# Gate and up projections of the feed-forward in two halves of 256 tokens, each with its own loads of the stationary weights

## The reference

```
x = x + groups @ w_out
h2 = rms_norm(x, g_ffn)
return x + (silu(h2 @ w_gate) * (h2 @ w_up)) @ w_down        # first block
...
gu = h @ w_in                                                # layers 0 to 3
return (silu(gu[..., :2816]) * gu[..., 2816:]) @ w_out
```

## Time and profile before

| | |
|---|---|
| median of 2 runs | 3288.5 us (3285.84 to 3291.16) |
| profiled execution, first to last instruction | 3288.7 us |
| instructions | 42736 |
| TensorE matmuls | busy 3220.8 us (98%), 15181 |
| TensorE weight loads | busy 2619.6 us (80%), 15181 |
| VectorE, ScalarE, GpSimd | busy 47%, 37%, 45% |
| memory traffic | 114 GB/s over the span |

### The profile page before, as it was taken

One profiled execution on the slowest core, in us unless ns is written; L12 is line 12 of the kernel. 1 busy time (PEld: TensorE's weight loads), 2 busy tenths in 40 slices (PEclk: granted clock), 3 DMA queues, 4 the chain that ended last, 5 costly groups with the idle time before them and its releaser, 6 DMA issues.

```text
span 3288.7 us, 42736 instructions
## 1 busy us (share of the span) xinstructions
PE 3220.8 (98%) x15181; PEld 2619.6 (80%) x15181; DVE 1549.8 (47%) x2615; ACT 1202.1 (37%) x1875; POOL 1480.9 (45%) x724
## 2 busy tenths in 40 slices
PE   8999999999999999999999999999999999999998
PEld 6876788888778888887888878877888877788886
DVE  2453355501145555467555224656556354752223
ACT  3455333222335332455432243125332243553322
POOL 3540554454235445524544454446444453154442
PEclk9999999999999999999999999999999999999999
DMA  4400155532224554211556333113555322032331
GB/s 161 122 26 1 65 204 191 202 106 93 68 65 160 193 202 145 84 59 63 180 191 208 105 96 96 39 33 103 204 191 188 103 90 77 5 99 96 96 103 64
DMA packets 103107, 376.12 MB, mean 114 GB/s; under 512 B 11456, under 2 KB 11584, under 8 KB 102848
## 3 DMA queue, kind: packets, MB, share of 16 engines
q1 hardware_dynamic: 102816, 373.86, 34.1%
q0 software_dynamic: 160, 0.52, 0.1%
HBM read 372.24 MB, written 2.10 MB: 114 GB/s over the span
## 4 chain that ended last, share of the span: by engine, by line
PE 52%; DVE 2%; ACT 1%; issue 1%; POOL 0%; DVEq 0%; ACTq 0%
PE bank L758 13%; PE bank L757 13%; PE bank L756 13%; PE bank L1362 2%; PE bank L859 1%; PE bank L854 1%; PE bank L855 1%; PE bank L808 1%; PE bank L809 1%; PE bank L810 1%; PE bank L1072 1%; PE bank L1328 1%; PE bank L1089 0%; PE bank L974 0%; PE bank L1258 0%
## 5 line engine op out<-in xcount | busy, mean ns | idle before, releaser
L623 POOL TENSOR_TENSOR w_lo<-raw,w_hi 128x1024 fp32r<-128x1024 f32 x501 | 1227.3, 2455 | 1368.2 <-ACT w_hi L1440 1368.0
L1440 ACT ACTIVATE w_hi<-raw 128x1024 fp32r<-128x1024 f32 x501 | 526.8, 1057 | 1183.2 <-PE bank L758 1022.4
L756 PE MATMUL bank<-h_hi,w_hi 128*128 128x512 f32 x2280 | 889.3, 390 | 0.0
L758 PE MATMUL bank<-h_hi,w_lo 128*128 128x512 f32 x2280 | 887.1, 389 | 0.0
L757 PE MATMUL bank<-h_lo,w_hi 128*128 128x512 f32 x2280 | 887.0, 389 | 0.0
L756 PEld LDWEIGHTS bank<-h_hi,w_hi 128*128 128x128 f32 x2280 | 427.9, 188 | 90.6 <-issue 2.0
L757 PEld LDWEIGHTS bank<-h_lo,w_hi 128*128 128x128 f32 x2280 | 427.9, 188 | 89.7 <-issue 1.0
L758 PEld LDWEIGHTS bank<-h_hi,w_lo 128*128 128x128 f32 x2280 | 427.9, 188 | 89.2
L2608 DVE CUSTOM_DVE_ANT_0 ada_raw<-ada_raw,cond_row 128x1024 f32<-128x1024 f32 x192 | 304.2, 1587 | 280.5 <-DMA ada_raw<-ada 270.6
L756 PE MATMUL bank<-hid_hi,w_hi 128*128 128x512 f32 x880 | 344.0, 391 | 0.0
L758 PE MATMUL bank<-hid_hi,w_lo 128*128 128x512 f32 x880 | 342.4, 389 | 0.0
(11 more groups left out here) (411 smaller groups left out, 4016.5 us busy)
## 6 DMA issues: line engine op xcount, KB each, us to landing
raw<-weights SPq DMA_DIRECT2D x501, 512.0 KB, 3.5
ada_raw<-ada SPq DMA_DIRECT2D x192, 512.0 KB, 4.3
layer_const<-layer_const SPq DMA_DIRECT2D x5, 512.0 KB, 3.6
x<-x_t SPq DMA_DIRECT2D x1, 2048.0 KB, 7.5
cond_row<-cond SPq DMA_DIRECT2D x4, 512.0 KB, 4.2
y_t<-x SPq DMA_DIRECT2D x8, 256.0 KB, 2.0
tables<-big_const SPq DMA_DIRECT2D x1, 768.0 KB, 5.9
cols<-columns SPq DMA_DIRECT2D x1, 569.5 KB, 8.4
```

The lines of the kernel that those rows point to most:

```text
L623: nc.gpsimd.tensor_tensor(w_lo[k % RING][:, :, :], raw[k % RING][:, :, :], w_hi[k % RING][:, :, :].bitcast(F32), ALU.subtract).then_inc(sm ...
L756: mm(out, w_hi[r][:, at, :], hi, start=first and at == 0, stop=False)
L758: op = mm(out, w_lo[r][:, at, :], hi, start=False, stop=last and at == len(pairs) - 1)
L1440: fn(w_hi[t % RING][:, :, :], raw[t % RING][:, :, :], ACT.Copy).then_inc(sm.hi_done, 1)
```

## The change

`m_tile` gets a flag `halved`, and `linear` passes it on in its loop of four tiles. `ffn` sets it for the gate and up tiles. With it, an output tile is computed in two halves of 256 tokens: for the first half all 8 chunks with their three matmuls each, then the same for the second half, into the two halves of the same bank. A tile then has 48 matmuls of 256 columns, each with its own load of a 128 x 128 stationary piece, in place of 24 of 512 columns. The waits at the head of the tile and the increment on its last matmul stay. The early tiles, the tile after the loop and all other projections keep the form of before.

```diff
-            def m_tile(k, mt, i, step, mt_step, hi, lo, chunks, parts_from=None):
+            def m_tile(k, mt, i, step, mt_step, hi, lo, chunks, parts_from=None, halved=False):
                 if mt >= 4:
                     pe.wait_ge(sm.lin_free, mt - 3 + mt_step * i)
+                if halved:
+                    pe.wait_ge(sm.lo_done, k + 1 + step * i)
+                    r = k % RING
+                    for t in range(2):
+                        tok = slice(256 * t, 256 * t + 256)
+                        out = bank[mt % 4][:, tok]
+                        for c in range(DT):
+                            mm(out, w_hi[r][:, c, :], hi[:, c, tok], start=c == 0, stop=False)
+                            mm(out, w_hi[r][:, c, :], lo[:, c, tok], start=False, stop=False)
+                            op = mm(out, w_lo[r][:, c, :], hi[:, c, tok], start=False, stop=c == DT - 1)
+                    op.then_inc(sm.slot_used, 1)
+                    return
...
-            def linear(tiles, hi, lo, chunks, after_second=None):
+            def linear(tiles, hi, lo, chunks, after_second=None, halved=False):
...
-                            m_tile(k + (done + q) * per, mt + done + q, i, 4 * per, 4, hi, lo, chunks)
+                            m_tile(k + (done + q) * per, mt + done + q, i, 4 * per, 4, hi, lo, chunks,
+                                   halved=halved)
...
-                linear(2 * FT - EARLY, h_hi, h_lo, [8])
+                linear(2 * FT - EARLY, h_hi, h_lo, [8], halved=True)
```

## The result

The changed kernel takes 3353.1 us (median of two runs, 3352.90 and 3353.35) against 3288.5 us, a ratio of 1.0192 with a 95% interval of 1.0162 to 1.0222. A second comparison gave 3354.3 us (median of 4) against 3290.2 us (median of 7), 1.0190 (1.0173 to 1.0207). So the change makes the kernel 1.9% slower, 64 us; the forecast was 3298 us with a range to 3340 us.

The account below looks back on a forecast made before the run. TensorE, busy for 98% of the span, was taken as the bound: matmul count times pace. 4800 x 1.9 ns = +9.1 us on 3288.7 us, other terms nothing, gave 3298 us; range 3283 to 3340 us, held at 0.80.

Parts of the forecast that it names:

- Step (1): In the loop of `linear`, 4800 matmuls of 512 columns (1088 us) become 9600 of 256 with 9600 loads.
- Step (2): In the halved loops, a 256-column stream takes 114.3 ns, two 228.6 ns: +1.9 ns for each replaced matmul.
- Step (3): In the halved loops, load and stream overlap, the longer sets the pace: max(114.3, 111.7) = 114.3 ns a half.
- Its lower bound: For a half in the loops: 106.7 ns, with none of the 13.4 ns over 512 columns; -64 us.
- The first rival: In the halved loops, array hand-over adds 13.4 ns to the load: 125.1 ns a half, 3401 us; 3354 or more, chance 0.09.
- Steps (4) and (5): In the halved loops, issue, waits, other engines' work and TensorE's doubled weight reads cost nothing, hidden behind TensorE.
- The load that comes too late by a little: In the halved loops, 2.6 ns of room is too little for the load; +113 us, 3354 or more at chance 0.09.
- its small form: A smaller lateness of the load in the halved loops: 116 to 120 ns a half, 3313 to 3352 us, chance 0.09.
- Load and stream in turns: In the halved loops, load and stream partly or wholly alternate: 169 or 226 ns a half, 3826 or 4370 us; chance 0.03.
- Instructions fetched again: At 45 backward jumps, the body of 384 loads and matmuls waits 2.5 us for a block: +112 us, 3401 us; chance 0.03.
- A half is cheaper than half: In the halved loops, 106.7 ns a half gives 3225 us; below 3283 us chance 0.03, over 2% faster 0.01.

Follow-up runs that it names:

- the quarters: The changed kernel with each tile in four pieces of 128 columns instead of two of 256, loads still of 128 columns: 4349.7 us.
- The 320- and 384-column trains: Runs of 24 equal-length matmuls in the changed kernel, tiles cut into 320 and 192 or 384 and 128 columns instead of 256 and 256: 3445.9 and 3576.1 us.

## Why the prediction was wrong

- **Step (1)**, 9600 matmuls of 256 for 4800 of 512: right, 3200 on each of the three new lines.
- **Step (2)**, the stream of a half at 114.3 ns, +1.9 ns for each replaced matmul: this is the step that failed, by its size. It measured 120.0 ns, +13.3 ns, which is 63.8 us where the sum had 9.1. The step took the price from a row with loads of half the width, said so, and costed that difference at nothing; the run with 256 columns behind loads of 64 shows 113.3 ns in these very loops, and only the full width of the load, with the rows written that go with it, brings it to 120.0.
- **Step (3)**, the longer of stream and load: right for the load (111.7 ns, the quarters) and right in that loads are not paid in full. Its lower bound named the 13.4 ns over 512 columns and asked only what would happen if a half had none of them. The reading next to it, that a half has all of them, was not made: 106.7 + 13.4 = 120.1 ns, and the result to within 1 us. The first rival did use the 13.4 ns, but on top of the load (125.1 ns). The plain f32 row (215 ns for 256 columns, little over twice 106.7) could be read as a small price, and it is of another number type.
- **Steps (4) and (5)**, issue, waits and memory at nothing: right. TensorE has no idle time in the loops, and the other engines keep their room.
- **The load that comes too late by a little** came nearest in size: its small form reached to 3352 us. It held that handing over new weights takes time, which fits a fixed price, but it put that time behind the load, where a longer stream would cover it. The 320- and 384-column trains pay in full with 35 and 62 ns of room, and the 192-column steps of 111.8 ns leave no room for a hand-over behind the load. Its point of decision, 120.2 ns, happens to lie beside the 120.0 that another cause made.
- **Load and stream in turns** is refuted: 120.0 ns is far under 169. The Trainium skill (TensorE: Matmul & The Clock Gate, Part 3, "The mechanism"), by whose rule loads on the same row groups do not overlap a matmul, differs from this trace after as before. The same section also has a load pulled ahead that goes into the background weight buffer; whether these loads do, the trace does not say.
- **Instructions fetched again** is refuted: at most two blocks in a whole loop, and no longer step at a turn. The row it rested on, no block on q8 in the first loop, came from a stretch that ends before the loop does; over the whole loop (413.4 to 631.0 us) there is one, as in the second. The rule of the Trainium skill on jumps (Runtime: NRT & Kernel Launch, "Instruction fetch mechanics") differs from the trace: the quarters' body of 768 loads and matmuls is longer than two blocks of 256 however it lies, and no turn stalls. The same section's store of 2048 instructions is in keeping with that, though no run shows its size.
- **A half is cheaper than half** is refuted by the same 120.0 ns.
- **The range.** It ended at 3340 us within a case that reached to 3352; with 120.1 ns as one of the bounds of step (2) it would have held the time.

## What to carry to other kernels

Before a stream is cut into shorter ones, take the running step apart into columns at the granted clock and a rest, and cost the cut with the whole rest paid again for each piece as well as with none of it. A row that serves as a price must match in number type, stream length and load width; if one of them differs, that difference is a bound of the range and not nothing. An engine that is busy for 98% of the span turns every nanosecond of an inner step into time: here 13 ns, 4800 times.

## What the runs showed of the hardware

- In float32r with 128 x 128 loads at the 2.4 GHz level a step takes 120.0, 146.4, 173.0 and 226.7 ns for 256, 320, 384 and 512 columns, and 111 to 112 ns for 128 and 192 (without the first steps of uneven trains).
- At 256 columns the price of a step falls with the width of its load, 13.3, 11.1, 9.3 and 6.6 ns for 128, 112, 96 and 64 columns; at 512 columns narrow loads are dearer than full ones (15.6 ns for 112, 16.7 ns for 64, 15.9 ns for 44, against 13.4).
- Loads of 64 columns can follow each other every 60.0 ns, loads of 128 columns every 111 to 112 ns.
- When short pieces alternate with long ones, the first long step behind the short train is longer and the first short step behind the long train shorter: 170 ns against 146.4 and 90 against 111.8 with 320 and 192 columns, 230 against 173.0 and 60 against 111.7 with 384 and 128.
